# Two layers of a hybrid decoder trunk on one core: where the first norm's reciprocal root is applied

## The reference

```
def rms_norm(x, w):
    xf = x.astype(jnp.float32)
    y = xf * lax.rsqrt(jnp.mean(xf * xf, axis=-1, keepdims=True) + EPS)
    return (y * w.astype(jnp.float32)).astype(x.dtype)

def mamba2_mixer(h, w_in, conv_w, conv_b, dt_bias, a_log, d_skip, norm_w, w_out):   # h = rms_norm(x, mix_norm[0])
    z, xbc, dt = _split(h @ w_in, [SSM_D_INNER, SSM_CONV_DIM, SSM_N_HEADS])
    xbc = jax.nn.silu(causal_dwconv(xbc, conv_w, conv_b))
    ...
    dt = jax.nn.softplus(dt.astype(f32) + dt_bias.astype(f32)).reshape(bsz, seq, g, hg)
    ...  # chunked scan, gated group norm, y @ w_out
```

## Time and profile before

| | |
|---|---|
| runs, median (lowest to highest) | 2667.74 us (2667.58 to 2672.6) |
| the profiled execution's own time | 2667.43 us |
| its span | 2665.7 us |
| PE busy | 2625.5 us, 98% of the span |
| DVE busy | 1788.8 us, 67% |
| ACT busy | 1429.2 us, 54% |
| POOL busy | 196.4 us, 7% |
| DMA | 481.94 MB, mean 181 GB/s |

### The profile page before, as it was taken

The page is one execution under the profiler, slowest core; times in us unless marked ns, Lnnn a source line. Parts: engine busy times, 40 slices in busy tenths (PEclk is TensorE's granted clock), DMA queues, the critical chain, the costliest instruction groups (busy, mean ns, idle before and its releaser), DMA issues. The chain is left out here.

```text
span 2665.7 us, 46463 instructions
## 1 busy us (share of the span) xinstructions
PE 2625.5 (98%) x15411; PEld 2292.3 (86%) x15411; DVE 1788.8 (67%) x2612; ACT 1429.2 (54%) x2210; POOL 196.4 (7%) x179
## 2 busy tenths in 40 slices
PE   7999999999999999999999999999999999999999
PEld 6888888888888888888888888888888888888888
DVE  7677777765677777775555756665677777775444
ACT  5676766654455555554444545555455555554443
POOL 0111111121200000000111000001300000000000
PEclk9999999999999999999999999999999999999999
DMA  5655555556555555556666565322555555556665
GB/s 185 218 191 194 191 191 185 193 171 189 180 184 188 188 187 187 188 187 188 189 187 195 175 197 191 103 95 93 183 181 189 189 189 188 189 188 183 188 188 168
DMA packets 135254, 481.94 MB, mean 181 GB/s; under 512 B 15104, under 2 KB 17152, under 8 KB 134160
## 3 DMA queue, kind: packets, MB, share of 16 engines
q1 hardware_dynamic: 132480, 467.72, 55.6%
q0 software_dynamic: 2336, 12.65, 1.4%
q10 hardware_dynamic: 368, 0.65, 0.1%
HBM read 478.80 MB, written 2.16 MB: 180 GB/s over the span
## 5 line engine op out<-in xcount | busy, mean ns | idle before, releaser
L969 DVE TENSOR_TENSOR w_lo<-raw,w_hi 128x1024 fp32r<-128x1024 f32 x900 | 1102.1, 1225 | 720.9 <-ACT w_hi L350 719.8
L682 PE MATMUL ps<-xn,w_hi 128*128 128x512 f32 x4768 | 1509.1, 398 | 17.3 <-DVE xn L995 10.7
L350 ACT ACTIVATE w_hi<-raw 128x1024 fp32r<-128x1024 f32 x900 | 938.7, 1044 | 889.5 <-PE ps L684 870.7
L684 PEld LDWEIGHTS ps<-xn,w_lo 128*128 128x128 f32 x4768 | 896.9, 188 | 212.2
L684 PE MATMUL ps<-xn,w_lo 128*128 128x256 f32 x4768 | 938.2, 278 | 0.0
L682 PEld LDWEIGHTS ps<-xn,w_hi 128*128 128x128 f32 x4768 | 728.4, 189 | 26.0 <-DVE xn L995 11.3
L682 PE MATMUL ps<-hid,w_hi 128*128 128x512 f32 x1408 | 446.9, 395 | 0.0
L684 PEld LDWEIGHTS ps<-hid,w_lo 128*128 128x128 f32 x1408 | 264.6, 188 | 57.1
L684 PE MATMUL ps<-hid,w_lo 128*128 128x256 f32 x1408 | 288.0, 279 | 0.0
L682 PEld LDWEIGHTS ps<-hid,w_hi 128*128 128x128 f32 x1408 | 219.6, 189 | 5.5
L682 PE MATMUL ps<-y_ssm,w_hi 128*128 128x512 f32 x512 | 161.6, 397 | 0.0
(11 more groups left out here) (238 smaller groups left out, 1762.9 us busy)
## 6 DMA issues: line engine op xcount, KB each, us to landing
raw<-w_gu SPq DMA_DIRECT2D x352, 512.0 KB, 3.8
raw<-w_ssm_in SPq DMA_DIRECT2D x162, 512.0 KB, 3.6
raw<-w_down SPq DMA_DIRECT2D x128, 448.0 KB, 3.4
raw<-w_nsa_in SPq DMA_DIRECT2D x82, 512.0 KB, 3.6
raw<-w_ssm_out SPq DMA_DIRECT2D x64, 512.0 KB, 4.5
raw<-w_down SPq DMA_DIRECT2D x64, 512.0 KB, 3.6
raw<-w_nsa_out SPq DMA_DIRECT2D x32, 512.0 KB, 4.0
wcum<-cum_scratch POOLq DMA_DIRECT2D x8, 1024.0 KB, 7.3
```

What stands on the lines that cost most here:

```text
L350: act.activation(w_hi[:, slot, 0:n * P], raw[:, slot, 0:n * P], ACT.Copy).then_inc(unit_rounded, 1)
L682: pe.matmul(acc[:, 0:2 * n], w_hi[:, slot, cols], x[:, kb, 0:2 * n], start=(kb == 0), stop=False)
L684: mm = pe.matmul(acc[:, n:2 * n], w_lo[:, slot, cols], x[:, kb, 0:n], start=False, stop=(kb == p.blocks - 1))
L969: TT(w_lo[:, slot, 0:n * P], raw[:, slot, 0:n * P], w_hi[:, slot, 0:n * P].bitcast(F32), ALU.subtract).then_inc(unit_split, 1)
```

## The change

Of the first norm only the weight is applied to x before the projection. ACT multiplies each of the 16 tiles by its weight and rounds it (128x256, one instruction), DVE forms the rest from `resid`, weight and rounded value (`weighted_rest`, moved up in the file). Both engines take, in this order, tiles 0 to 7, unit 0, tiles 8 to 15, unit 1, then units 2 and 3. SP issues two quarters of x, unit 0, two quarters, unit 1. The squares move from DVE to POOL. PE does units 0 and 1 first and sums the squares between the first units (`first_sums`). ACT's root comes in `dt_body`, behind the rounding of units 4 and 5; DVE's reciprocal behind their splits. The `dt` tile and the 80 tiles of `ssm` are multiplied by `rstd` afterwards; for dt the bias is then added by an instruction of its own.

```diff
-        for name in ("gu0", "gates", "kvc", "kvs", "q", "gu1"):
+        for name in ("ssm", "gu0", "gates", "kvc", "kvs", "q", "gu1"):
             SCALED[ph[name].tile0] = n_scaled
             n_scaled += ph[name].tiles
...
+            p = ph["dt"]
+            for v in range(p.body):
+                for c in (2 * v, 2 * v + 1):
+                    sp.dma_start(resid[:, 4 * c:4 * c + 4], x_in[:, 4 * c:4 * c + 4]).then_inc(x_landed[c], 16)
+                sp.dma_start(raw[:, v], p.dram[0, :, v * UNIT * P:(v + 1) * UNIT * P]).then_inc(raw_landed[v], 16)
+            for name in order[1:]:
                 load(ph[name])
...
-            for w in range(RING):
+            act.wait_ge(consts_landed, 32)
+            for v in range(2):
+                for m in range(8 * v, 8 * v + 8):
+                    act.wait_ge(x_landed[m // 4], 16)
+                    act.activation(xn[:, m, 0:T], resid[:, m], ACT.Copy, scale=norm_weight(0, m)).then_inc(xn_rounded, 1)
+                round_unit(v, unit_sizes[v])
+            for w in range(2, RING):
                 round_unit(w, unit_sizes[w])
-            act.wait_ge(eps_set, 1)
-            act.wait_ge(consts_landed, 32)
-            stream_norm(0, norm_a)
...
                 take_cross(p, 0, 0)
+                act.wait_ge(eps_set, 1)
+                stream_std(0)
                 act.activation(hc[:, 1:2], hc[:, 1:2], ACT.Exp).then_inc(a_exp, 1)
                 act.wait_ge(tile_out, 1)
...
-            pe.wait_ge(ones_set, 1)
-            for c in range(4):
+            def first_sums(c):
+
                 pe.wait_ge(xsq_ready, c + 1)
                 for m in range(4):
                     mm = pe.matmul(ps[2][:, 0:T], ones[:], xsq[c][:, m * T:(m + 1) * T], start=(c + m == 0), stop=(c + m == 6))
-            mm.then_inc(ssum_done, 1)
+                if c == 3:
+                    mm.then_inc(ssum_done, 1)
+
+            pe.wait_ge(ones_set, 1)
+            pe.wait_ge(ident_set, 1)
             gemm_first(0, ph["dt"])
-            pe.wait_ge(ident_set, 1)
+            first_sums(0)
...
+                    elif v == 0:
+                        first_sums(1)
+                        first_sums(2)
+                    elif v == 1:
+                        first_sums(3)
                     elif v == 12:
                         turn_dt()
...
-            for c in range(4):
-                x = resid[:, 4 * c:4 * c + 4].rearrange("p a t -> p (a t)")
-                dve.wait_ge(x_landed[c], 16)
-                TT(xsq[c], x, x, ALU.mult).then_inc(xsq_ready, 1)
-            for w in range(RING):
+            dve.wait_ge(consts_landed, 32)
+            for v in range(2):
+                for m in range(8 * v, 8 * v + 8):
+                    dve.wait_ge(x_landed[m // 4], 16)
+                    weighted_rest(0, m)
+                split_unit(v, unit_sizes[v])
+            for w in range(2, RING):
                 split_unit(w, unit_sizes[w])
-            dve.wait_ge(consts_landed, 32)
-            stream_norm(0, norm_a)
...
+                stream_rstd(0)
                 dve.wait_ge(cross_copied, 1)
-                STT(h[0], ps[0][0:HEADS, 0:T], hc[:, 0:1], cross[0:HEADS, 0], ALU.add, ALU.add).then_inc(tile_out, 1)
+                link(TT(h[0], ps[0][0:HEADS, 0:T], cross[0:HEADS, 0], ALU.add))
+                link(TT(h[0], h[0], rstd[0:HEADS], ALU.mult))
+                TS(h[0], h[0], hc[:, 0:1], None, ALU.add).then_inc(tile_out, 1)
...
+            for c in range(4):
+                x = resid[:, 4 * c:4 * c + 4].rearrange("p a t -> p (a t)")
+                pool.wait_ge(x_landed[c], 16)
+                pool.tensor_tensor(xsq[c], x, x, ALU.mult).then_inc(xsq_ready, 1)
```

More of the change, by code:

```diff
@@ L281, in trunk @@
         NORM_OF = {ph["gu0"].tile0: 1, ph["gates"].tile0: 2, ph["gu1"].tile0: 3}
-        XN_READY = [4, 4 + D_TILES, 4 + 2 * D_TILES, 4 + 3 * D_TILES]
+        XN_READY = [D_TILES * (n + 1) for n in range(4)]
         def norm_weight(n, m):
@@ L319, in load @@
                 loop(sp, 0, p.n, body)
-            for c in range(4):
-                sp.dma_start(resid[:, 4 * c:4 * c + 4], x_in[:, 4 * c:4 * c + 4]).then_inc(x_landed[c], 16)
-            for name in order:
+            p = ph["dt"]
[4 more added lines that the diff above has]
+            for name in order[1:]:
                 load(ph[name])
@@ L363, in stream_std @@
                 act.activation(rstd[:], ps[2][:, 0:T], ACT.Sqrt, scale=1.0 / (D_TILES * P), bias=eps[:, 0:1]).then_inc(std_ready, 1)
-            def stream_norm(n, scratch):
-                act.wait_ge(ssum_done, n + 1)
-                act.activation(rstd[:], ps[2][:, 0:T], ACT.Sqrt, scale=1.0 / (D_TILES * P), bias=eps[:, 0:1]).then_inc(std_ready, 1)
-                for k in range(4):
-                    act.wait_ge(norm_y, 4 * n + k + 1)
-                    act.activation(xn[:, 4 * k:4 * k + 4, 0:T], scratch[k % 2][:], ACT.Copy).then_inc(xn_rounded, 1)
-            for w in range(RING):
+            act.wait_ge(consts_landed, 32)
[5 more added lines that the diff above has]
+            for w in range(2, RING):
                 round_unit(w, unit_sizes[w])
-            act.wait_ge(eps_set, 1)
-            act.wait_ge(consts_landed, 32)
-            stream_norm(0, norm_a)
             def dt_body(i, nxt):
@@ L714, in gemm_first @@
                     if v < 2:
-                        pe.wait_ge(xn_ready, 2 * v + 2 if n == 0 else XN_READY[n] - D_TILES // 2 * (1 - v))
+                        pe.wait_ge(xn_ready, XN_READY[n] - D_TILES // 2 * (1 - v))
                     gemm_unit(p, 0, v, xn)
@@ L985, in stream_rstd, with weighted_rest @@
                 dve.wait_ge(rstd_ready, n + 1)
-            def stream_norm(n, scratch):
-                dve.wait_ge(std_ready, n + 1)
-                dve.reciprocal(rstd[:], rstd[:]).then_inc(rstd_ready, 1)
-                dve.wait_ge(rstd_ready, n + 1)
-                name = "ffn_norm" if n % 2 else "mix_norm"
-                def rest(k):
-                    dve.wait_ge(xn_rounded, 4 * n + k + 1)
-                    TT(xn[:, 4 * k:4 * k + 4, T:2 * T], scratch[k % 2][:], xn[:, 4 * k:4 * k + 4, 0:T].bitcast(F32), ALU.subtract).then_inc(xn_ready, 1)
-                for k in range(4):
-                    if k == 2:
-                        dve.wait_ge(xn_ready, 4 * n + 2)
-                    for c in range(4):
-                        m = 4 * k + c
-                        last = STT(scratch[k % 2][:, c], resid[:, m], col(name, n // 2 * D_TILES + m), rstd[:], ALU.mult, ALU.mult)
-                    last.then_inc(norm_y, 1)
-                    if k % 2:
-                        rest(k - 1)
-                        rest(k)
+            def weighted_rest(n, m):
+                flat = lambda a: a.rearrange("p o t -> p (o t)")
+                dve.wait_ge(xn_rounded, XN_READY[n] - D_TILES + 1 + m)
+                STT(flat(xn[:, bass.ds(m, 1), T:2 * T]), flat(resid[:, bass.ds(m, 1)]), norm_weight(n, m),
+                    flat(xn[:, bass.ds(m, 1), 0:T]).bitcast(F32), ALU.mult, ALU.subtract).then_inc(xn_ready, 1)
             dve.memset(eps[:, 0:1], EPS)
```

21 lines of the change are left out of this document (7 added, 14 removed).

## The result

The changed kernel takes 2692.73 us (median of 4 runs, 2691.55 to 2702.86) against 2667.66 us (4 runs, 2667.56 to 2672.6): ratio 1.0095, 95% interval 1.0083 to 1.0107. It is slower by 25 us, where 7 were forecast and 2679.5 us was the upper end. The direction was right, the size was not.

A forecast was written before the change was run, and what follows sets the result against it. PE was taken to bound the kernel, working 2625.5 of 2665.7 us. To 2667.43 us the prediction added 6.4 for unit 15's delay, 1.0 for the clock and 0 for the other multiplications: 2674.8 us, range 2668 to 2679.5.

The forecast's parts named there:

- Step 6: In the groups: the other 75 ssm multiplications, 4.3 us of VectorE work a group, cost PE 0.
- the cover: VectorE's idle time in each group, 15 us, taken to hide the added multiplications.
- Step 1: At the start: POOL's squares and VectorE's rests exclude each other; PE's first unit comes at 17.9 us, against 26.16.
- Rival E: In seven groups: multiplications cost 0.7 us each, besides the main forecast's losses; 2679.7 us, chance 0.08.
- Step 5: Behind the transposition: PE's 3.2 us wait brings a stretch at half clock, costing 1.0 us (0 to 1.7).
- Steps 1 to 4: The start up to unit 15: the first unit's gain goes to sums and waits; unit 15 comes 6.4 us later.
- S: When PE gets its first unit: 17.9 us, against 26.16 before.
- T: When PE finishes the last sum of squares: S + 20.0 = 37.9 us.
- step 4: VectorE behind unit 6: five multiplications add 2.15 us, PE waits 3.2 us at the transposition, unit 15 at 77.9 us.
- B: At the start: POOL and VectorE don't exclude each other, or only half; S 13.0 to 16, 2669.0 us, chance 0.18.
- D: At the start: B's S, and VectorE's chains of step 4 don't bind; 2662.8 us, chance 0.08.
- C: At the start: a POOL square costs 2.44 us, S = 20.0; 2676.9 us with the clock, chance 0.16.

The follow-up runs named there:

- Sum first: Changed kernel, VectorE's tile sum and multiplication behind unit 17 moved ahead of scan_rest, which releases POOL: 2684.18 us, ratio 1.0046 to the kernel before.
- selects first: Changed kernel, POOL's two affine selects moved ahead of its wait for the convolution and the last group's output: 2689.31 us, ratio 1.0078 to the kernel before.
- all, selects first: Changed kernel with "Sum first", "late squares", "transposition later", "selects first", units 6 and 7 ahead of the root, a later SiLU: 2668.42 us, ratio 0.9991.
- transposition later: Changed kernel, PE's transposition behind unit 16 instead of 14, ScalarE's copy of it two steps later: 2689.46 us, ratio 1.0068 to the kernel before.
- multiplications only: Kernel before the change, its 80 ssm tiles multiplied by rstd a second time, start untouched: 2689.47 us, ratio 1.0071.
- change without them: Changed kernel without the multiplications of the 80 ssm tiles by rstd, dt tile keeping its own: 2673.31 us, ratio 1.0016 to the kernel before.
- late squares: Changed kernel, POOL's four squares waiting until two units are split: 2690.65 us, ratio 1.0081 to the kernel before.

## Why the prediction was wrong

**Step 6 failed.** It priced 75 multiplications at nothing, "the cover is 15 us of idle time a group". They cost 14.9 us, on average 2.1 us in each of seven groups. The cover was an average over a group; what counted was VectorE's order at one place, where the earlier trace rows had already shown a split and a POOL multiplication exclude each other. Step 1 used that rule for the start, and step 6 didn't carry it to the seven other places with the same neighbours. It also looked for harm only in the splits; PE waited for the scan's arrays, which had 2.7 us (wcum) and 3.5 us (xw) to spare before the change and no ring to run ahead in. "Sum first" and "selects first" show what took the place of the cover: 8.9 us by the held multiplication, 5.2 by the splits held behind the selects; and in "all, selects first" the same multiplications cost nothing. Rival E, given 0.08, had the place and a third of the price.

**Step 5 was too small.** It took 1.0 us, at most 1.7; "transposition later" gives 2.4 (5.4 less 3.0). The row for it, the unit of 4.24 us behind 1.83 us of idle time, was a shorter wait; behind 2.99 us unit 15 took 5.3. Two further rows of the same place show how the price grew: behind 1.4 us of waiting (multiplications only) unit 15 took 2.89 us and nothing more was lost, behind 2.28 us (change without them) 4.24, and with the next unit 1.5 us were lost.

**Steps 1 to 4 held, the first in part by luck.** S was 17.33 us for 17.9, by the lock ("late squares" gives 13.16 without). But step 1 had the third quarter of x land at 10.1 us and nobody wait for it; POOL waited for it until 11.43, so the last square ended at 15.4 us instead of 14.3, and in the pause five rests got through instead of one. The two errors nearly cancel. The others: T 37.9 as forecast; the wait at unit 6 2.57 for 2.5; the wait at the transposition 2.99 for 3.2; unit 15 at 78.26 for 77.9. Five multiplications in step 4 were 2.15 us: with and without them unit 15 differs by 2.6 us. The old slack of 1.0 us also shows: alone, they cost 1.4 of their 2.15.

**The rivals.** B and D, no exclusion: refuted by the rests. C, squares of 2.44: refuted by 1.9 to 2.1. Of the missing 16.8 us (24.2 less 7.4), step 6 has 14.9, step 5 1.5 and steps 1 to 4 0.4.

## What to carry to other kernels

A small VectorE instruction is priced by what it stands beside: where it reads two tiles in SBUF and can start just behind a wide GpSimd instruction, it costs that one's length, and so does all that hangs on it. So look up every place in the loop where the two meet, and issue what the other engines wait for ahead of the instruction that releases GpSimd. Idle time on an average hides nothing from a chain with 3 us to spare; and work taken off PE's critical start (squares to ScalarE, 16 sums to 4, GpSimd out of the start) was worth another 9 us.
